# Short TensorE products spread singly among the long ones in a two-block transformer kernel

## The reference

```
first:   h = x + 0.5 * swiglu(rms_norm(x))          # 1024 -> 2816 gate and up -> 1024
         h = h + mixer(rms_norm(h))                 # MoBA attention + stick-breaking attention
         h = h + 0.5 * swiglu(rms_norm(h));  final rms_norm
second:  the same frame; mixer = forgetting attention (fox) + sparse attention (dsa):
         score = sum over 8 index heads of w * relu(q_idx . k_idx); the top 64 keys of a row are kept
both mixers: out = (sigmoid(ga) * (o_a @ w_a) + sigmoid(gb) * (o_b @ w_b)) @ w_out
```

## Time and profile before

| | |
|---|---|
| time, median of 3 runs | 1117.95 us (1117.80 to 1118.03) |
| time of the profiled execution | 1117.82 us |
| its span | 1116.0 us |
| TensorE busy, products | 1110.3 us, 99%, 5854 of them |
| TensorE busy, weight loads | 944.4 us, 85% |
| VectorE busy | 786.0 us, 70% |
| ScalarE busy | 621.3 us, 56% |
| granted TensorE clock | 1.0 on average |
| DMA | 208.02 MB, mean 186 GB/s |

### The profile page before, as it was taken

One profiled execution on the slowest core, in us unless ns is written; L12 is line 12 of the kernel. 1 busy time (PEld: TensorE's weight loads), 2 busy tenths in 40 slices (PEclk: granted clock), 3 DMA queues, 4 the chain that ended last, 5 costly groups with the idle time before them and its releaser, 6 DMA issues.

```text
span 1116.0 us, 14890 instructions
## 1 busy us (share of the span) xinstructions
PE 1110.3 (99%) x5854; PEld 944.4 (85%) x5854; DVE 786.0 (70%) x1112; ACT 621.3 (56%) x825; POOL 57.7 (5%) x105
## 2 busy tenths in 40 slices
PE   9999999999999999999999999999999999999998
PEld 8888888888888888888888888888888788888887
DVE  6777754766887677775477787557898686777752
ACT  6556542677566455564346556337787854656540
POOL 1000000100000000000000000021343000000000
PEclk9999999999999999999999999999999999999999
DMA  9765565644454656655565555557643455665550
GB/s 317 250 189 189 190 244 190 209 158 144 162 193 157 207 188 189 189 189 189 189 208 187 190 189 189 189 154 256 223 146 122 150 176 166 189 190 193 191 180 38
DMA packets 142581, 208.02 MB, mean 186 GB/s; under 512 B 9296, under 2 KB 100584, under 8 KB 142512
## 3 DMA queue, kind: packets, MB, share of 16 engines
q1 hardware_dynamic: 139408, 198.07, 54.1%
q0 software_dynamic: 3088, 9.00, 2.4%
q10 hardware_dynamic: 16, 0.00, 0.0%
HBM read 205.98 MB, written 2.65 MB: 187 GB/s over the span
## 4 chain that ended last, share of the span: by engine, by line
PE 96%; ACT 2%; DVE 1%; issue 1%; DMA 0%; SPq 0%; DVEq 0%
PE banks L1800 27%; PE banks L1686 16%; PE banks L1688 16%; PE banks L1687 16%; PE banks L1797 14%; PE banks L1758 1%; PE banks L2031 1%; PE banks L1708 1%; PE banks L1976 1%; ACT w_hi L751 0%; DMA raw<-in_ffn_w_gate 0%; PE banks L2061 0%; DVE w_lo L1138 0%; PE banks L2009 0%; PE banks L2058 0%
## 5 line engine op out<-in xcount | busy, mean ns | idle before, releaser
L1138 DVE TENSOR_TENSOR w_lo<-raw,w_hi 128x2048 fp32r<-128x2048 f32 x186 | 422.8, 2276 | 167.0 <-ACT w_hi L751 166.6
L751 ACT ACTIVATE w_hi<-raw 128x2048 fp32r<-128x2048 f32 x186 | 352.2, 1897 | 111.9 <-PE banks L1688 108.2
L1800 PE MATMUL banks<-xT,w_hi 128*128 128x512 f32 x1344 | 314.3, 390 | 0.0
L1800 PEld LDWEIGHTS banks<-xT,w_hi 128*128 128x128 f32 x1344 | 249.3, 188 | 49.8
L1797 PEld LDWEIGHTS banks<-xT,w_lo 128*128 128x128 f32 x1344 | 167.4, 191 | 4.1 <-DVE xg L1152 0.7
L1686 PE MATMUL banks<-w_hi,xT 128*128 128x512 f32 (+1 forms) x432 | 170.4, 394 | 0.0
L1797 PE MATMUL banks<-xT,w_lo 128*128 128x256 f32 x1344 | 169.8, 283 | 0.2
L1688 PE MATMUL banks<-w_hi,xT 128*128 128x512 f32 (+1 forms) x432 | 166.9, 386 | 0.0
L1687 PE MATMUL banks<-w_lo,xT 128*128 128x512 f32 (+1 forms) x432 | 166.7, 386 | 0.0
L1686 PE MATMUL banks<-w_hi,hT_hi 128*128 128x512 f32 x352 | 137.3, 390 | 0.0
L1688 PE MATMUL banks<-w_hi,hT_lo 128*128 128x512 f32 x352 | 137.0, 389 | 0.0
(11 more groups left out here) (315 smaller groups left out, 902.6 us busy)
## 6 DMA issues: line engine op xcount, KB each, us to landing
raw<-in_ffn_w_gate SPq DMA_DIRECT2D x88, 512.0 KB, 3.9
raw<-in_ffn_w_up SPq DMA_DIRECT2D x88, 512.0 KB, 4.9
raw<-in_ffn_w_down SPq DMA_DIRECT2D x88, 512.0 KB, 4.3
raw<-in_w_in SPq DMA_DIRECT2D x76, 512.0 KB, 4.5
raw<-in_w_out SPq DMA_DIRECT2D x16, 512.0 KB, 4.2
raw<-in_w_branch_moba SPq DMA_DIRECT2D x4, 512.0 KB, 4.2
raw<-in_w_branch_sb SPq DMA_DIRECT2D x4, 512.0 KB, 5.2
raw<-in_w_branch_a SPq DMA_DIRECT2D x4, 512.0 KB, 4.3
```

The source lines that it names most:

```text
L751: act.activation(w_hi[u % SLOTS][:, 0:n], raw[u % RAWS][:, 0:n], ACT.Copy).then_inc(hi_done, 1)
L1138: dve.tensor_tensor(w_lo[r][:, 0:n], raw[r][:, 0:n], w_hi[u % SLOTS][:, 0:n], ALU.subtract).then_inc(lo_done, 1)
L1800: m = pe.matmul(bank[b + s], mh, xT[:, k].rearrange("p a s -> p (a s)"), start=first, stop=k == KC - 1, skip_group_check=c == 0)
```

## The change

Every function that issued a row of short products becomes a generator that issues one and yields. A `between` function is called ahead of each long product and takes one step. In a mixer's slot the first long products now have ahead of them the scores that stood at the end of the slot before, and the last long products have this slot's transpositions. `head_pair`, `sb_sum` and `sum_rows` stay in a row at the slot's end. At the seams `turn_x`, `turn_merged` and `turn_hidden` are spread in the same way. `turn_x` of quarter 1 of M0, F2 and M1 moves into the phase before; quarter 3 moves from before to within the second batch of 12; in F1 and F3 quarter 2 and quarter 3 move into the 16 long products. No product is added or taken away.

```diff
+            def spaced(short, first):
+                return lambda i: next(short, None) if i >= first else None
...
-                turn_x(ph, 1)
-                batch(0, 0)
-                for q in range(2, 4):
-                    turn_x(ph, q)
-                batch(0, 1)
-                batch(1, 0)
-                batch(1, 1)
+                for tt, hf in Q_FFN:
+                    short = turn_x(ph, 2 + hf) if tt == 0 else None
+                    batch(tt, hf, spaced(short, 8) if short else None)
...
@@ first_pairs (F1, F3)
-                turn_x(ph, 2)
                 pe.wait_ge(lo_done, u + 1)
                 pe.wait_ge(xT_hi_done, x0 + 2)
                 for p in range(2):
                     if p:
                         pe.wait_ge(gained, 4 * GAIN_OF[ph] + 4)
                     pair_products(ph, 0, 0, p, True)
-                turn_x(ph, 3)
                 pe.wait_ge(xT_lo_done, x0 + 2)
                 for p in range(2):
-                    m = pair_products(ph, 0, 0, p, False)
+                    short = turn_x(ph, 2 + p)
+                    m = pair_products(ph, 0, 0, p, False, spaced(short, 0))
...
@@ ffn, last down chunk
-                        if d == NCH - 1 and q == 3 and ph in NEXT:
-                            turn_x(NEXT[ph], 0)
+                        turns = spaced(turn_x(NEXT[ph], q - 2), 2) if d == NCH - 1 and q >= 2 and ph in NEXT else None
...
@@ mixer
+                for slot in range(4, 44):
                     j, q = divmod(slot, 4)
+                    late, turns, first = scores_of(slot - 1), turns_of(slot), 12 - count_turns(slot)
+
+                    def between(i):
+                        if not next(late, False) and i >= first:
+                            next(turns, False)
+
                     if j < PROJ:
-                        project(j, q // 2, q % 2)
-                    elif slot < 44:
-                        branch(0, q)
+                        project(j, q // 2, q % 2, between)
+                    else:
+                        branch(0, q, between)
+                    rest_of(late)
+                    rest_of(turns)
...
-                        if it.kind == "SM" and d == SM_AT["turn"]:
-                            turn_probs(it)
-                        if it.kind == "TR" and d == 0:
-                            turn(it)
...
-                        if it.kind in ("SM", "SB", "IX") and d == 0:
-                            scores(it)
...
-                turn_merged(0)
-                turn_merged(1)
-                branch(1, 3)
+                branch(1, 3, spaced(two_turned(turn_merged, 0), 0))
                 output(0, 0, 0)
-                turn_merged(2)
-                turn_merged(3)
-                output(0, 0, 1)
+                output(0, 0, 1, spaced(two_turned(turn_merged, 2), 0))
                 for n, hf in ((0, 1), (1, 0), (1, 1)):
                     output(n, hf, 0)
-                    if (n, hf) == (1, 1):
-                        turn_x(NEXT[ph], 0)
-                        turn_x(NEXT[ph], 1)
-                    output(n, hf, 1)
+                    turns = two_turned(lambda q: turn_x(NEXT[ph], q), 0)
+                    output(n, hf, 1, spaced(turns, 0) if (n, hf) == (1, 1) else None)
```

More of the change, by code:

```diff
@@ L1683, in _, with three, rest_of @@
         def _(pe):
-            def three(dst, st, hi, lo, mhi, mlo, start, stop):
+            def three(dst, st, hi, lo, mhi, mlo, start, stop, between=None, i=0):
+                if between:
+                    between(i)
                 pe.matmul(dst, st(hi), mhi, start=start, stop=False)
+                if between:
+                    between(i + 1)
                 pe.matmul(dst, st(hi), mlo, start=False, stop=False)
+                if between:
+                    between(i + 2)
                 return pe.matmul(dst, st(lo), mhi, start=False, stop=stop)
+            def spaced(short, first):
+                return lambda i: next(short, None) if i >= first else None
+            def rest_of(short):
+                for _ in short:
+                    pass
             def rows(u, width, k4, col=0, n=NB):
@@ L1693, in rows, with four @@
                 return w_hi[u % SLOTS][:, o:o + n], w_lo[u % RAWS][:, o:o + n]
-            def four(u, tt, dst, k0, first, last, n=NB, hi=xT_hi, lo=xT_lo):
+            def four(u, tt, dst, k0, first, last, n=NB, hi=xT_hi, lo=xT_lo, between=None):
                 for k4 in range(4):
@@ L1699, in four @@
                     m = three(dst, lambda z, k=k0 + k4: z[:, k, tt * P:(tt + 1) * P], hi, lo, mh, ml,
-                              first and k4 == 0, last and k4 == 3)
+                              first and k4 == 0, last and k4 == 3, between, 3 * k4)
                 return m
@@ L1822, in pair_chunk @@
                 if c == 1 and ph not in FIRST_OF:
[L1823 removed]
+                    rest_of(spread_rows(ph))
                 for p in range(2):
@@ L1844, in first_chunk @@
                 pe.wait_ge(xT_lo_done, 4 * PREP_OF[ph] + quarters(ph).index((tt, hf)) + 1)
-                m = four(u, tt, bank[tt][:], 4 * hf, hf == 0, hf == 1)
+                m = four(u, tt, bank[tt][:], 4 * hf, hf == 0, hf == 1, between=between)
                 if tt == 1:
@@ L2078, in project @@
                             pe.wait_ge(gated, 2 * (j - 7))
-                    m = four(u, tt, bank[2 * (j % 2) + tt][:, 0:n], 4 * hf, hf == 0, hf == 1, n)
+                    m = four(u, tt, bank[2 * (j % 2) + tt][:, 0:n], 4 * hf, hf == 0, hf == 1, n, between=between)
                     if tt == 1:
@@ L2128, in turn_merged, with two_turned, output @@
                                            xg[:, tt, n * NB + k * P:n * NB + (k + 1) * P], ident)
-                    ins.then_inc(m_turned, 1)
-                def output(n, hf, tt):
+                        if k == 3:
+                            ins.then_inc(m_turned, 1)
+                        yield True
+                def two_turned(turn, q):
+                    yield from turn(q)
+                    yield from turn(q + 1)
+                def output(n, hf, tt, between=None):
                     u = u0 + 24 + 2 * n + hf
@@ L2134, in output @@
                     pe.wait_ge(mT_lo, 4 * b + Q_MIX.index((tt, hf)) + 1)
-                    m = four(u, tt, bank[2 * n + tt][:], 4 * hf, hf == 0, hf == 1)
+                    m = four(u, tt, bank[2 * n + tt][:], 4 * hf, hf == 0, hf == 1, between=between)
                     if tt == 1:
```

71 lines of the change are left out of this document (51 added, 20 removed).

## The result

The kernel after takes 1126.43 us (median of 4 runs, 1126.23 to 1126.45); the kernel before, beside it on the same chip, 1117.99 us (4 runs, 1117.8 to 1118.13). The ratio is 1.0075, with a 95% interval of 1.0058 to 1.0093. The forecast was 1126.3 us. The profiled execution has a span of 1124.6 us where before had 1116.0, at a granted clock of 1.0 in both.

A forecast was written before the change was run, and what follows sets the result against it. TensorE's own work, 96% of the chain of waits, was taken as the bound. 2.4 + 0.6 + 2.6 + 0.2 + 0.6 + 1.5 + 1.1 - 0.5 = 8.5 us on 1117.8 gave 1126.3, range 1116.5 to 1131.5.

The forecast's parts named there:

- Lone transpositions: TensorE's stream: a transposition costs 0.121 us alone against 0.109 in a row, 202 x 0.012 = 2.4 us more.
- rival (b): Stream as dear as now, new waits fall away, long products behind runs slightly slow now: 1121.3 us, chance 0.28.
- Lone scores: 96 score products of 128 columns cost 0.112 us alone or in a row: nothing, from 5.2 less to 0.6 more.
- rival (a): A lone short product hides its own load and the next one's under the long products: 1099 us, chance 0.07.
- Cover behind head outputs: Transpositions no longer follow the eight head-output products, so cover of about 0.07 goes in nine places: 0.6 us.
- F1 and F3: Start of both phases: uncovered run 0.45, later quarter 0.25, new wait 0.5, ScalarE's delay 0.1: 2.6 us, from 1 to 4.
- Starts of M0, F2 and M1: TensorE waits for the first quarter, 0.2 us for three starts; ScalarE's 2.7 delay costs M1 0.6, from 0 to 1.6.
- wait near 766: At M1's start products would wait for a weight unit from VectorE's late subtraction: 0.6 us, between 0 and 1.6.
- Later scores in M1: Later indexer scores delay ScalarE and VectorE's head norms, so transpositions near 795 wait: 1.5 us, from 0 to 2.3.
- Transpositions that wait already: Waits at 804.93 and 824.84 grow by 0.7 and 0.4 as transpositions move earlier: 1.1 us together, from 0 to 1.6.
- Given back in M0: Head 2's scores wait 0.6 us for a rounded key; TensorE arrives later and waits less: -0.5 us.

The follow-up runs named there:

- e2_scores_back: The kernel after with the scores alone moved back, in a row at the end of their own slot; 1124.77 us, ratio 1.0062.
- e5_turns_back: The kernel after with the mixer slots' transpositions alone moved back into rows at the slot's end, scores still spread and late; 1124.35 us, ratio 1.0058.
- x3: The kernel before with 480 more products of 128 columns, in 40 rows of 12 where nothing waits; 1173.87 us.
- x4: The kernel before with 480 more products of 128 columns, each alone ahead of a long product; 1172.48 us.
- e3_pairs_back: The kernel after with quarters 2 and 3 at F1's and F3's start back in rows, quarter 2 ahead of the wait; 1123.61 us, ratio 1.0051.
- b1: The kernel before with each head's scores in M0 in a row behind the next slot's third long product; 1117.32 us against 1117.85, ratio 0.9995.
- x1: The kernel before with 480 more transpositions, in 40 rows of 12 ahead of long products where nothing waits; 1172.4 us.
- x2: The kernel before with 480 more transpositions, each alone ahead of a long product where nothing waits; 1173.45 us.

## Why the prediction was right

The mechanism and the time were right: each short product exposes one load wherever it stands, and the new waits came where they were forecast. But several sizes were off, and the misses cancelled. Point by point:

- **Lone transpositions, 2.4: mis-sized in its parts, too high.** The lone one was right (0.118 and 0.116 measured, 0.121 forecast); the one in a row was taken too cheap. Measured from the long product before a group to the eighth behind it, less 0.227 for each long product, at places without a wait or another short product near (medians): rows of four take 0.479 us in the kernel before (7 places) and 0.498 spread in the kernel after (11); eight together 0.891 (9) and 0.952 (4). A head's three take 0.840 with its four scores in a row behind them (e2_scores_back, 7) where all seven in a row take 0.817 (8). That is 0.005 to 0.008 each, so 260 make about 1.8 us (an estimate: 68 counted as fours, 72 as threes, the rest as eights). The prediction read the row only to its second long product (0.45) and left out the slow tail, 0.027, which it then named under rival (b). Its upper bound for a lone one halves 0.227 to 0.107; it is 0.114.
- **Lone scores, 0: wrong, 1.1.** The prediction put this term at nothing, from one row of four. Four scores in a row take 0.464 over the long products' own time (8 places), spread 0.518 (e5_turns_back, 7). In e5_turns_back only the scores are spread in the slots, so what TensorE loses there beyond its waits is their price: 0.35 us in M0 (0.26 later from 209 to 343 us, while the wait for the rounded key is 0.09 shorter) and 0.78 in M1 (2.13 later from 770 to 898, of which the waits hold 1.35). In x3 and x4, far from rows of mixed sizes, there was no such cost; why it is there in the mixers no run shows. The trace also has 160 scores, 80 of them of 128 columns, and not 192 and 96: the bounds of 5.2 and 0.6 should have been 4.3 and 0.5, and rival (a) 1100.
- **Cover behind head outputs, 0.6: a little high.** In M1 the outputs with three transpositions took 1.29 us over the long products around them and take 1.36, from 888.47 to 890.96 (2.49 less five of 0.227): 0.07 more, of which the three spread transpositions are 0.023 by the medians above, so some 0.04 for a place and 0.4 for nine. It wasn't tried by itself.
- **F1 and F3, 2.6: too low, 3.2.** In each stage the second eight low products start 0.13 us later than the stage before left them (0.84 late at 380.99, 0.71 before; 0.25 was forecast for the later quarter). The run that is now behind that wait, and the spreading, cost 0.5 up to the next low products (0.45). The new wait there is 0.51 (0.5). The low products behind it lose 0.08 more. All that is as forecast within 0.1. But ScalarE's delay cost 0.38 and not 0.1. The delay itself was read well: ScalarE loses 3.1 in the stage (3.85 less 0.71) against TensorE's 1.2 (1.94 less 0.71), where 3 and 1.2 were forecast. The slack was not: at the gate the kernel before has 1.47 to spare (392.81 to 394.28), not 1.7 to 1.8. e3_pairs_back took 3.0 of these 3.2 away from the two stages.
- **Starts of M0, F2 and M1, 0.2 and 0.6: too high.** From F1's running to 766 us TensorE falls back by 0.3 us (2.32 to 2.62), and the list of waits has none there. The wait near 766 did not come:

```profile
765.98 2.29 DVE L1138 TENSOR_TENSOR w_lo<-raw,w_hi 128x2048 fp32r<-128x2048 f32 x1 [2.07 <-ACT w_hi L751]
...
768.66 0.39 PE L1691 MATMUL banks<-w_lo,xT 128*128 128x512 f32 x1
```

  The subtraction of the earlier trace rows starts 3.66 later, TensorE comes 2.62 later: 1.04 of the slack of 1.12 is used up, and 0.1 is left. The step that failed is "ScalarE makes good about 1 us of the 2.7": at its eviction of run 3 it is 2.5 behind TensorE (5.13 late, at 756.81 for 751.68, less 2.6), and it made good 1.5.
- **Later scores in M1, 1.5: right.** A wait of 1.33 from start to start and a step of 1.4. e2 and e5 show that it is made of both edits.
- **Transpositions that wait already, 0.7 and 0.4: right in sum.** From start to start the waits are 1.25 for 0.25 and 0.63 for 0.37, so 1.0 and 0.26 more. The reason given for the first ("moved 0.91 earlier") is one of two that would each do.
- **Given back in M0, 0.5: two thirds.** The wait for the rounded key is 0.42 instead of 0.76 from start to start (0.3 and 0.6 in the list). b1 shows that it can go altogether.

The waits, from start to start, add up to 2 x (0.50 + 0.51 + 0.38) (the last quarter's, the turned quarter's, the gate's) + 1.33 + 1.00 + 0.26 - 0.34 = 5.0 us (forecast: 5.5, the lines from F1 on), and 0.2 belongs to the execution. Of the 8.64 us of the span, 3.4 are then left for the stream, where the prediction had 3.0 and the terms above give 1.8 + 1.1 + 0.4 = 3.3. Counted so, the scores were 1.1 too low, the lone transpositions 0.6 and the starts 0.8 too high, and six misses of some 0.2 each add 0.4. The close hit rests on that cancelling.

## What to carry to other kernels

On a stream where each short product costs one exposed weight load, alone or in a row, spreading them hides nothing and costs a little (some 0.006 us for a transposition, 0.03 for a head's four scores here). What counts more is when the group is complete and when its first member must wait. In this kernel a group that another engine evicts as a whole was better as a row, as late as its inputs ask and as early as its reader needs, and ahead of a wait rather than behind it. When the engines fall back together, compare how late each is against TensorE at every hand-over with what was to spare there: an engine without gaps makes nothing good.

## What the runs showed of the hardware

A transposition of 128 x 128 costs 0.109 us within a row, but the row leaves the next seven long products 0.027 us slower in sum (x1: 40 rows alike), so 0.114 in rows of twelve (x1), 0.120 in rows of four (the kernel before), 0.116 to 0.118 alone (x2, and the kernel after at 225.07). The Trainium skill, page "TensorE: Matmul & The Clock Gate", speaks in the table at its head of weight loads pulled ahead of products in flight; here, in all 480 places of x2, the load of a long product starts 1 to 2 ns after the short product ahead of it starts, so one load is held ahead and never two. And a longer busy time of a group can mean nothing: 480 transpositions are listed with 59.0 us in rows and 129.8 us alone, at 1.1 us between the two kernels. Groups by line and shape in x1_turn_row, then in x2_turn_lone:

```profile
L1923 PE MATMUL banks<-const 128*128 128x128 f32 x480 | 59.0, 273 | 0.0
```
```profile
L1926 PE MATMUL banks<-const 128*128 128x128 f32 x480 | 129.8, 270 | 0.0
```
